# Layer norm tiles shared with GpSimd and ScalarE, and the first chunk's products of the upper halves put ahead of those of the lower halves

## The chip, the cores and the metric

One core of a Trainium2 chip runs the kernel. The metric is the device time of one execution in microseconds (us), the median of a few runs; lower is better. The engines work side by side, each through its own list of instructions, and meet at semaphores: TensorE (PE; its weight loads PEld), VectorE (DVE), ScalarE (ACT), GpSimd (POOL) and SyncE (SP, which issues the DMAs).

## The reference

Two transformer blocks of two layers each, on 256 tokens of width 1024. The change lies in the layer norms of the second block, and in the matmul that follows each of them (it also touches the matmul behind the RMS norms of the first block):

```python
def _layer_norm(x, g, b):
    xf = x.astype(jnp.float32)
    mu = jnp.mean(xf, axis=-1, keepdims=True)
    var = jnp.mean(jnp.square(xf - mu), axis=-1, keepdims=True)
    return ((xf - mu) * lax.rsqrt(var + LN_EPS) * g + b).astype(x.dtype)
...
    for l in range(DEPTH):
        x = _layer_norm(DN_ALPHA * x + 0.5 * _swiglu(x, ffn1_w1[l], ffn1_w2[l]), ln1_g[l], ln1_b[l])
        mix = _token_mix(x, w_in[l], ...)
        x = _layer_norm(DN_ALPHA * x + mix, ln2_g[l], ln2_b[l])
        x = _layer_norm(DN_ALPHA * x + 0.5 * _swiglu(x, ffn2_w1[l], ffn2_w2[l]), ln3_g[l], ln3_b[l])
```

The last of the six layer norms has no matmul behind it and is written elsewhere, so five are concerned.

## The kernel before

The tokens lie along the free dimension: `x[:, k, 0:256]` is tile k of eight (KT = 8), 128 model columns by 256 tokens in float32. All matmuls are made in float32r from halves: each operand is the sum of an upper half (rounded) and a lower half (what the rounding left), and a product takes three matmuls: upper weight with upper operand, upper weight with lower operand, lower weight with upper operand (`three`).

The weights come in chunks of 1 MB through a ring in SBUF. For each chunk ScalarE rounds it to `w_hi` (`round_next`, two halves of 1024 columns), VectorE makes the rest `w_lo` (`rest_next`, `rest_half`), and TensorE runs 48 matmuls over it. `w_hi` and `w_lo` hold two chunks, so chunk c+2 can be rounded once TensorE is done with chunk c.

A layer norm stands at the start of a stage; the mean, the squares and the root `rs` (the reciprocal of the standard deviation, 128x256, the same in all partitions) were made at the end of the stage before, by `Moments`. In `layer_norm` VectorE multiplies each tile with the gain and the root (`scaled_x`); ScalarE adds the bias and rounds to the upper half (`upper`); VectorE makes the lower half (`lower`); and after the eight tiles ScalarE adds the bias in place (`affine`). VectorE's list is written out as: tiles 0, 1, 2, then lower half 0, tile 3, lower half 1, and so on. TensorE runs the first chunk of the stage in `pe_side_by_side`: two output tiles side by side, and for each k the six matmuls of that tile as soon as its lower half is there.

Two kinds of stages begin so: `project_and_compress` (twice) and `ffn_stage` (three times). What ScalarE does next is, in the first, two copies of chunk 0's result out of PSUM and the rounding of chunk 2; in the second, the load of the table for Silu, the gate of chunk 0 and the rounding of chunk 2. The chunks 0 and 1 were rounded ahead.

In the first block the stage `glu_stage` (twice) starts with `model_norm`, and its first chunk runs through `pe_side_by_side` too; there GpSimd makes the upper halves and VectorE the lower ones.

Of the kernel before, what the change touches and what calls it, by code (L numbers as in the profile page):

```python
# [26 lines left out]
P = 128  # L27
D = 1024
KT = D // P
# [88 lines left out]
def build(nc, wstream, xT, ctxT, cT, consts, vecs, rpb, rel, out):  # L118
    ctx = ExitStack()
    with ctx:  # L120
# [80 lines left out]
        rows_turned = count("rows_turned")  # L201
        modulated = count("modulated")
        total_squares = count("total_squares")
        late_consts = count("late_consts")
        values_taken = count("values_taken")
        values_turned = count("values_turned")
# [117 lines left out]
                        mm.then_inc(half_read.sem, 1)  # L324
            mm.then_inc(chunk_done.sem, 1)

        def pe_side_by_side(pe, hi, lo, before, tok=S):

            pe_acc(pe, 0, 0)
            pe_half(pe, 0, 0, 1)  # L330
            for k in range(KT):
                before(k)
                for m in range(2):
                    mm = three(pe, acc(0, tok, m * 512), slice((m * KT + k) * P, (m * KT + k + 1) * P), g0[0] % 2,
                               hi(k), lo(k), k == 0, k == KT - 1)
            mm.then_inc(chunk_done.sem, 1)

        def pe_in_parts(pe, j, hi, lo, before, out):
# [231 lines left out]
        class Norm:  # L570
# [1 line left out]

            def __init__(self, pe, act, dve, before):
                self.pe, self.act, self.dve, self.before = pe, act, dve, before

        def model_norm(mod, scales, scratch):

            m0, u0, l0, s0 = mixed.n, upper.n, lower.n, scaled_x.n  # L580
            model_hi, model_lo = model_halves()

            def act_steps(act):
                for k in range(KT):
                    act.wait_ge(scaled_x.sem, s0 + k + 1)
                    for w in range(2):
                        v = scratch(k)[:, w * S:w * S + S]
                        o = act.activation(v, v, ACT.Identity, scale=scales[:, k, w:w + 1], bias=mod[:, k, w:w + 1])
                    o.then_inc(mixed.sem, 1)
                round_next(act, 0, 0)  # L590

            def pool_steps(pool):
                for k in range(KT):
                    pool.wait_ge(mixed.sem, m0 + k + 1)
                    pool.tensor_copy(model_hi[:, k, :], scratch(k)).then_inc(upper.sem, 1)

            def dve_steps(dve):
                for n in range(KT + 3):
                    if n < KT:
                        dve.tensor_tensor(scratch(n), x[:, n, :], rs[:], ALU.mult).then_inc(scaled_x.sem, 1)  # L600
# [9 lines left out]
            n = Norm(None, act_steps, dve_steps, lambda pe, k: pe.wait_ge(lower.sem, l0 + k + 1))  # L610
            n.pool = pool_steps
            return n

# [63 lines left out]
        def layer_norm(layer, which):  # L677

            gains, biases = par(layer, f"ln{which}_g"), par(layer, f"ln{which}_b")
            r0, s0, u0, l0 = rooted.n, scaled_x.n, upper.n, lower.n  # L680
            c = g0[0] + 1

            def src(k):
                return x[:, k, 0:S]

            def act_steps(act):
                for k in range(KT):
                    act.wait_ge(scaled_x.sem, s0 + k + 1)
                    act.activation(x_hi[:, k, 0:S], src(k), ACT.Identity, bias=biases[:, k:k + 1]
                                   ).then_inc(upper.sem, 1)  # L690
                for k in range(KT):
                    act.wait_ge(lower.sem, l0 + k + 1)
                    act.activation(src(k), src(k), ACT.Identity, bias=biases[:, k:k + 1]).then_inc(affine.sem, 1)

            def dve_steps(dve):
                dve.wait_ge(rooted.sem, r0)
                for n in range(KT + 2):
                    if n < KT:
                        dve.scalar_tensor_tensor(out=src(n), in0=src(n), scalar=gains[:, n:n + 1], in1=rs[:, 0:S],
                                                 op0=ALU.mult, op1=ALU.mult).then_inc(scaled_x.sem, 1)  # L700
                    k = n - 2
                    if 0 <= k < KT:
                        dve.wait_ge(upper.sem, u0 + k + 1)
                        dve.scalar_tensor_tensor(out=x_lo[:, k, 0:S], in0=src(k), scalar=biases[:, k:k + 1],
                                                 in1=x_hi[:, k, 0:S].bitcast(F32), op0=ALU.add, op1=ALU.subtract
                                                 ).then_inc(lower.sem, 1)
                rest_half(dve, c, 0, 1)

            for count_ in (scaled_x, affine, upper, lower):
                count_.n += KT  # L710
            return Norm(None, act_steps, dve_steps, lambda pe, k: pe.wait_ge(lower.sem, l0 + k + 1))

        scored = count("scored")
        sunk = count("sunk")
# [670 lines left out]
        def glu_stage(layer, pads, glu_gate, tok, norm, na_bias):  # L1385
# [11 lines left out]
            with nc.Block() as block:  # L1397
# [11 lines left out]
                @block.tensor  # L1409
                def _(pe):  # L1410
                    hi, lo = model_operand(tok)
                    keep_awake(pe, 9, 1536)
                    for j in range(n):
                        if j:
                            pe_columns(pe, j // 2, j % 2, hi, lo, tok)
                        else:
                            pe_side_by_side(pe, hi, lo, lambda k: norm.before(pe, k), tok)
# [404 lines left out]
        def ffn_stage(layer, norm, more=True, bias=None):  # L1822
# [10 lines left out]
            with ExitStack() as st:  # L1833
# [20 lines left out]
                with nc.Block() as block:  # L1854
# [7 lines left out]
                    def _(pe):  # L1862
# [4 lines left out]

                        def up_chunk(i, s):
                            if norm and first(i, s):
                                pe_side_by_side(pe, hi, lo, lambda k: norm.before(pe, k))  # L1870
# [98 lines left out]

                    @block.gpsimd  # L1970
                    def _(pool):
                        def chunk(i, s):
                            j = 2 * i + s
                            pool.wait_ge(acc_free.sem, g0[0] + s + 1 + 2 * i)
                            pool.tensor_copy(h_hi[:, j, :], hid[:, s, :]).then_inc(upper.sem, 1)  # L1975
                            pool.wait_ge(upper.sem, h0 + s + 1 + 2 * i)
                            pool.tensor_tensor(h_lo[:, j, :], hid[:, s, :], h_hi[:, j, :].bitcast(F32),  # L1977
                                               ALU.subtract).then_inc(lower.sem, 1)
                        pairs_of(pool, chunk)
# [462 lines left out]
        def project_and_compress(layer, plan, norm, kkc, vc, v_b, gates, st):  # L2442
# [44 lines left out]
            with nc.Block() as block:  # L2487
# [19 lines left out]

                @block.gpsimd
                def _(pool):
                    pool.memset(both[:].bitcast(F32), 0.0).then_inc(gpart.sem, 1)  # L2510
                    earlier = iter([(gpart.sem, gb + 1)] + [(values_flat.sem, f0 + k) for k in range(1, 8)])
                    flatten(pool, range(2, 4), values_flat, lambda: next(earlier))

                @block.tensor
                def _(pe):
# [22 lines left out]
                    for j, (kind, o, _) in enumerate(plan[:n]):  # L2538
                        if kind == "r":
                            pe_rows(pe, j // 2, j % 2, S, 256)  # L2540
                        elif j == 0:
                            pe_side_by_side(pe, *model_operand(S), lambda k: norm.before(pe, k))
# [517 lines left out]
```

## Time and profile before

| | us |
|---|---|
| median of 3 runs | 2368.11 (2368.05 to 2371.05) |
| the profiled execution | 2366.44 |
| its span in the trace | 2364.7 |

The profiled execution is 1.67 us below the median of the runs; its span is 1.74 us shorter than its time, which is what lies around the program. The mean granted TensorE clock was 0.997 of full speed. In the rows further down a time of the timeline counts from the start of the span; `x3` is three instructions that follow each other on an engine, with the time of all; what stands in brackets is how long the engine sat idle before, and what ended the wait.

### The profile page before, as it was taken

Reading aid. Unit: us, or ns where it says so; the run is one execution under the profiler, and the core shown is the slowest. Engines: PE = TensorE matmul, PEld = TensorE weight load, DVE = VectorE, ACT = ScalarE, POOL = GpSimd, SP = SyncE. Lnnn points to the kernel's source line nnn. Section 1 sums busy time; section 2 is a strip of 40 time slices with the busy share of each in tenths; the row PEclk is TensorE's granted clock in tenths of the full one; section 3 lists DMA queues with packets and bytes.
Section 4 is the critical chain, followed back from the end, with each engine's and each line's share of the span. In section 5 each row is a group of like instructions: output and inputs, shape, how many; then the busy total and the mean of one; then the engine's idle time right before and its main releaser. Section 6 shows DMA issues by size and latency. Waiting matters only on the chain. (4 is left out here: it accounts for less than half of the span.)

```text
span 2364.7 us, 45036 instructions
## 1 busy us (share of the span) xinstructions
PE 2275.5 (96%) x17296; PEld 2054.3 (87%) x17296; DVE 1498.9 (63%) x2663; ACT 1191.2 (50%) x1934; POOL 244.1 (10%) x272
## 2 busy tenths in 40 slices
PE   6999999999989999999999899999999998999998
PEld 3777677788878689999988899999999988999998
DVE  5487974453567875656476766665665577667654
ACT  6344743643345556434366555543544566555443
POOL 0012000000012000023010100131131001000320
PEclk9999999999999999999999999999999999999999
DMA  7321023434233035555554335455455453344552
GB/s 292 122 74 61 2 107 145 168 151 160 89 123 116 19 125 182 193 196 195 195 176 154 132 138 183 163 191 195 159 195 196 161 192 139 126 161 162 194 195 89
DMA packets 61844, 355.61 MB, mean 150 GB/s; under 512 B 6208, under 2 KB 19712, under 8 KB 20352
## 3 DMA queue, kind: packets, MB, share of 16 engines
q1 hardware_dynamic: 61552, 353.55, 41.7%
q8 instruction: 102, 1.67, 0.3%
q14 instruction: 46, 0.38, 0.1%
q10 hardware_dynamic: 144, 0.01, 0.0%
HBM read 349.29 MB, written 1.10 MB: 148 GB/s over the span
## 5 line engine op out<-in xcount | busy, mean ns | idle before, releaser
L257 DVE TENSOR_TENSOR w_lo<-ring,w_hi 128x1024 fp32r<-128x1024 f32 x638 | 812.3, 1306 | 441.1 <-ACT w_hi L243 440.6
L299 PE MATMUL psum<-halves,w_hi 128*128 128x256 f32 (+1 forms) x3314 | 1003.9, 303 | 12.7 <-DVE halves L604 3.7
L301 PE MATMUL psum<-halves,w_lo 128*128 128x256 f32 (+1 forms) x3314 | 985.4, 297 | 0.0
L300 PE MATMUL psum<-halves,w_hi 128*128 128x256 f32 (+1 forms) x3314 | 984.4, 297 | 0.0
L243 ACT ACTIVATE w_hi<-ring 128x1024 fp32r<-128x1024 f32 (+1 forms) x638 | 644.0, 1049 | 301.4 <-PE psum L301 134.5
L299 PEld LDWEIGHTS psum<-halves,w_hi 128*128 128x128 f32 x3314 | 624.1, 188 | 48.9 <-issue 11.5
L300 PEld LDWEIGHTS psum<-halves,w_hi 128*128 128x128 f32 x3314 | 624.3, 188 | 25.7 <-issue 1.7
L301 PEld LDWEIGHTS psum<-halves,w_lo 128*128 128x128 f32 x3314 | 623.6, 188 | 23.6
L1900 PE MATMUL psum<-h_hi,w_hi 128*128 (+1 forms) x640 | 176.6, 276 | 0.0
L1902 PE MATMUL psum<-h_lo,w_hi 128*128 (+1 forms) x640 | 176.6, 276 | 0.0
L1903 PE MATMUL psum<-h_hi,w_lo 128*128 (+1 forms) x640 | 176.6, 276 | 0.0
L1924 ACT ACTIVATE gate<-psum 128x256 f32<-128x256 f32 x88 | 33.9, 385 | 258.2 <-PE psum L301 258.2
L906 ACT ACTIVATE probT<-psum 128x512 f32<-128x512 f32 (+3 forms) x128 | 79.5, 621 | 149.1 <-PE psum L821 149.1
L1975 POOL CAST h_hi<-hid 128x256 f32 (+1 forms) x88 | 35.1, 399 | 994.8 <-DVE hid L1944 994.8
L921 ACT ACTIVATE prob<-prob,neg 128x256 f32<-128x256 f32 (+6 forms) x256 | 127.6, 502 | 19.2 <-DVE neg L874 18.1
L1900 PEld LDWEIGHTS psum<-h_hi,w_hi 128*128 128x128 f32 x640 | 120.1, 188 | 0.0
L1902 PEld LDWEIGHTS psum<-h_lo,w_hi 128*128 128x128 f32 x640 | 120.1, 188 | 0.0
L1903 PEld LDWEIGHTS psum<-h_hi,w_lo 128*128 128x128 f32 x640 | 120.1, 188 | 0.0
L1944 DVE SCALAR_TENSOR_TENSOR hid<-psum,gate 128x256 f32<-128x256 f32 x88 | 37.3, 424 | 125.5 <-ACT gate L1924 125.5
L1977 POOL TENSOR_TENSOR h_lo<-hid,h_hi 128x256 f32 (+1 forms) x88 | 111.2, 1264 | 13.5 <-POOL h_hi L1975 12.7
L1521 DVE SCALAR_TENSOR_TENSOR conv_out<-cpad,vec,conv_out 128x512 f32<-128x512 f32 (+1 forms) x180 | 108.6, 668 | 0.0
L821 PEld LDWEIGHTS psum<-cst,prob 128*128 128x128 f32 (+1 forms) x544 | 57.4, 138 | 48.8 <-DVE prob L881 39.5
(334 smaller groups left out, 2922.0 us busy)
## 6 DMA issues: line engine op xcount, KB each, us to landing
ring<-wstream SPq DMA_DIRECT2D x320, 1024.0 KB, 4.8
x<-xT SPq DMA_DIRECT2D x2, 1024.0 KB, 7.5
x<-ctxT SPq DMA_DIRECT2D x2, 1024.0 KB, 10.1
rel_bias<-bias_by_distance SPq DMA_DIRECT2D x2, 1024.0 KB, 7.5
fox_bias<-forgetting_sums SPq DMA_DIRECT2D x2, 1024.0 KB, 7.5
cst<-consts SPq DMA_DIRECT2D x1, 1534.0 KB, 11.7
wk<-wk_once SPq DMA_DIRECT2D x8, 128.0 KB, 4.4
kk_sw<-kk_sw SPq DMA_DIRECT2D x8, 128.0 KB, 5.7
```

Of the source, the lines that this page charges most:

```text
L243: act.activation(w_hi[:, c % 2, h], ring[:, (c + 2 * i) % RING, h], ACT.Copy).then_inc(hi_done.sem, 1)
L257: dve.tensor_tensor(w_lo[:, c % 2, h], ring[:, (c + 2 * i) % RING, h], w_hi[:, c % 2, h].bitcast(F32), ALU.subtract).then_inc(split_done.s ...
L299: pe.matmul(o, w_hi[:, c, w_cols], hi, start=first, stop=False)
L300: pe.matmul(o, w_hi[:, c, w_cols], lo, start=False, stop=False)
L301: return pe.matmul(o, w_lo[:, c, w_cols], hi, start=False, stop=last)
L906: act.activation(self.probT[0:w, v % self.TURNS, :, 0:n], psum[0:w, at:at + wide].rearrange("p (h k) -> p h k", h=2)[:, :, 0:n], ACT.Copy) ...
L921: o = act.activation(p, p, ACT.Exp, bias=self.neg[:, t % 3, half:half + 1], accum_out=self.den[:, t % 3, half:half + 1])
L1521: dve.scalar_tensor_tensor(out=o, in0=src, scalar=wc, in1=o, op0=ALU.mult, op1=ALU.add).then_inc(conv_step.sem, 1)
L1900: pe.matmul(o, w_hi[:, c, b:b + P], h_hi[:, kt, :], start=start and k == 0, stop=False)
L1902: pe.matmul(o, w_hi[:, c, b:b + P], h_lo[:, kt, :], start=False, stop=False)
L1903: mm = pe.matmul(o, w_lo[:, c, b:b + P], h_hi[:, kt, :], start=False, stop=False)
L1977: pool.tensor_tensor(h_lo[:, j, :], hid[:, s, :], h_hi[:, j, :].bitcast(F32), ALU.subtract).then_inc(lower.sem, 1)
```

## The change

VectorE scales tiles 0 to 4 as before. GpSimd multiplies tiles 5, 6 and 7 with the root, ScalarE then multiplies each of them with the gain (in place) and waits for its own result before it rounds the tile. In `pe_side_by_side` the four matmuls that need only the upper half of tile n (upper and lower weights, two output tiles) come as soon as that upper half is there, and the two that need the lower half of tile n-1 come behind them. That function also serves the two stages with `model_norm`.

```diff
         def pe_side_by_side(pe, hi, lo, norm, tok=S):
+            c = g0[0] % 2
...
             pe_acc(pe, 0, 0)
             pe_half(pe, 0, 0, 1)
-            for k in range(KT):
-                before(k)
-                for m in range(2):
-                    mm = three(pe, acc(0, tok, m * 512), slice((m * KT + k) * P, (m * KT + k + 1) * P), g0[0] % 2,
-                               hi(k), lo(k), k == 0, k == KT - 1)
+            for n in range(KT + 1):
+                if n < KT:
+                    norm.rounded(pe, n)
+                    for m in range(2):
+                        o = acc(0, tok, m * 512)
+                        pe.matmul(o, w_hi[:, c, columns_of(m, n)], hi(n), start=n == 0, stop=False)
+                        pe.matmul(o, w_lo[:, c, columns_of(m, n)], hi(n), start=False, stop=False)
+                k = n - 1
+                if k >= 0:
+                    norm.rest_made(pe, k)
+                    for m in range(2):
+                        mm = pe.matmul(acc(0, tok, m * 512), w_hi[:, c, columns_of(m, k)], lo(k), start=False,
+                                       stop=k == KT - 1)
             mm.then_inc(chunk_done.sem, 1)
...
         def layer_norm(layer, which):
...
+            OWN = 5
...
+            def pool_steps(pool):
+                pool.wait_ge(rooted.sem, r0)
+                for k in range(OWN, KT):
+                    pool.tensor_tensor(src(k), src(k), rs[:, 0:S], ALU.mult).then_inc(rooted_x.sem, 1)
+
             def act_steps(act):
                 for k in range(KT):
-                    act.wait_ge(scaled_x.sem, s0 + k + 1)
+                    if k < OWN:
+                        act.wait_ge(scaled_x.sem, s0 + k + 1)
+                    else:
+                        act.wait_ge(rooted_x.sem, o0 + k - OWN + 1)
+                        act.activation(src(k), src(k), ACT.Copy, scale=gains[:, k:k + 1]).then_inc(gained.sem, 1)
+                        act.wait_ge(gained.sem, n0 + k - OWN + 1)
                     act.activation(x_hi[:, k, 0:S], src(k), ACT.Identity, bias=biases[:, k:k + 1]
                                    ).then_inc(upper.sem, 1)
...
             def dve_steps(dve):
                 dve.wait_ge(rooted.sem, r0)
                 for n in range(KT + 2):
-                    if n < KT:
+                    if n < OWN:
                         dve.scalar_tensor_tensor(out=src(n), in0=src(n), scalar=gains[:, n:n + 1], in1=rs[:, 0:S],
                                                  op0=ALU.mult, op1=ALU.mult).then_inc(scaled_x.sem, 1)
...
@@ -1969,6 +2001,9 @@
                     @block.gpsimd
                     def _(pool):
+                        if norm:
+                            norm.pool(pool)
+
...
@@ -2507,6 +2542,7 @@
                 @block.gpsimd
                 def _(pool):
+                    norm.pool(pool)
                     pool.memset(both[:].bitcast(F32), 0.0).then_inc(gpart.sem, 1)
```

ScalarE's list at the start of the first `project_and_compress`, before (L689 makes the upper halves, `halves`; L693 is the bias in place; L2597 takes chunk 0's result out of PSUM; L243 rounds a half chunk):

```order
L689 ACTIVATE halves<-x,vec 128x256 [waits scaled_x] x8
L693 ACTIVATE x<-x,vec 128x256 [waits lower] x8
L2597 ACTIVATE x<-psum 64x2x256 [waits acc_free,chunk_done]
L2598 ACTIVATE x<-psum 64x2x256
L243 ACTIVATE w_hi<-ring 128x1024 [waits chunk_done,landed_odd]
```

and now (L715 is the rounding, L713 the gain, L719 the bias):

```order
L715 ACTIVATE halves<-x,vec 128x256 [waits scaled_x] x5
L713 ACTIVATE x<-x,vec 128x256 [waits rooted_x]
L715 ACTIVATE halves<-x,vec 128x256 [waits gained]
L713 ACTIVATE x<-x,vec 128x256 [waits rooted_x]
L715 ACTIVATE halves<-x,vec 128x256 [waits gained]
L713 ACTIVATE x<-x,vec 128x256 [waits rooted_x]
L715 ACTIVATE halves<-x,vec 128x256 [waits gained]
L719 ACTIVATE x<-x,vec 128x256 [waits lower] x8
L2633 ACTIVATE x<-psum 64x2x256 [waits acc_free,chunk_done]
```

Three instructions came in ahead of the last three roundings, each with a wait of ScalarE for itself behind it, and all that follows them stands behind them.

VectorE's list at the same place, now (L725 scales a tile, L730 makes a lower half; before, three more of the scalings alternated with the lower halves behind these):

```order
L725 SCALAR_TENSOR_TENSOR x<-x,vec,rs 128x256 [waits rooted]
L725 SCALAR_TENSOR_TENSOR x<-x,vec,rs 128x256 x2
L730 SCALAR_TENSOR_TENSOR halves<-x,vec,halves 128x256 [waits upper]
L725 SCALAR_TENSOR_TENSOR x<-x,vec,rs 128x256
L730 SCALAR_TENSOR_TENSOR halves<-x,vec,halves 128x256 [waits upper]
L725 SCALAR_TENSOR_TENSOR x<-x,vec,rs 128x256
L730 SCALAR_TENSOR_TENSOR halves<-x,vec,halves 128x256 [waits upper] x6
L258 TENSOR_TENSOR w_lo<-ring,w_hi 128x1024 [waits hi_done]
```

and GpSimd's, now (before, the memset was its first work there; in `ffn_stage` its first work was a cast behind the first gate):

```order
L2543 UNCONDITIONAL_BRANCH [waits barrier_Pool_Activation_PE_DVE_SP_gather]
L705 TENSOR_TENSOR x<-x,rs 128x256 [waits rooted]
L705 TENSOR_TENSOR x<-x,rs 128x256 x2
L2546 MEMSET both 128x4096
L2518 TENSOR_TENSOR flat<-x,vec 64x120 [waits gpart,doubled]
```

The first five scalings stand where they stood; GpSimd's three multiplications wait for the same semaphore as VectorE's first scaling, so both engines begin at once, and both read tiles of `x` and the root from SBUF.

## Rows read from the trace of the kernel before

**Rows 1.** Stretches: window; length; busy us of PE, PEld, DVE, ACT, POOL; granted clock; DMA.

```profile
1202.10:1212.00 9.90, 9.57 (x78) 9.35 (x79) 7.59 (x19) 7.86 (x18) 3.52 (x1) 1.00 0.41 133
...
2167.30:2177.30 10.00, 9.70 (x78) 9.48 (x79) 7.56 (x17) 8.00 (x17) 0.00 (x0) 1.00 0.40 125
...
1504.00:1590.00 86.00, 86.00 (x761) 86.00 (x760) 52.55 (x48) 38.64 (x50) 27.04 (x32) 1.00 0.53 194
```

**Rows 2.** Timeline of VectorE, second layer norm (a `ffn_stage`): start, duration.

```profile
1494.59 1.28 DVE L699 SCALAR_TENSOR_TENSOR x<-x,vec,rs 128x256 f32<-128x256 f32 x3 [0.91 <-PEq L2280]
...
1496.98 0.47 DVE L699 SCALAR_TENSOR_TENSOR x<-x,vec,rs 128x256 f32<-128x256 f32 x1
...
1499.75 1.27 DVE L704 SCALAR_TENSOR_TENSOR halves<-x,vec,halves 128x256 fp32r<-128x256 f32 x3
1500.93 1.22 DVE L257 TENSOR_TENSOR w_lo<-ring,w_hi 128x1024 fp32r<-128x1024 f32 x1
...
1506.26 2.90 DVE L257 TENSOR_TENSOR w_lo<-ring,w_hi 128x1024 fp32r<-128x1024 f32 x2 [0.53 <-ACT w_hi L243]
```

**Rows 3.** Timeline of ScalarE, the same stage.

```profile
1499.86 0.51 ACT L689 ACTIVATE halves<-x,vec 128x256 fp32r<-128x256 f32 x1 [0.29 <-DVE x L699]
1500.28 3.29 ACT L693 ACTIVATE x<-x,vec 128x256 f32<-128x256 f32 x8
1503.59 1.28 ACT L1924 ACT_TABLE_LOAD   x1
...
1505.17 2.00 ACT L243 ACTIVATE w_hi<-ring 128x1024 fp32r<-128x1024 f32 x2
```

**Rows 4.** Timeline of TensorE, the same stage: tile 5, chunk 1's first, chunk 2's first.

```profile
1500.30 0.37 PE L299 MATMUL psum<-halves,w_hi 128*128 128x256 f32 x1
...
1502.43 0.28 PE L317 MATMUL psum<-halves,w_hi 128*128 128x262 f32 x1
...
1507.87 0.28 PE L299 MATMUL psum<-halves,w_hi 128*128 128x256 f32 x1
```

**Rows 5.** Timeline of three engines, first layer norm (a `project_and_compress`); last: chunk 2's first matmul.

```profile
1202.19 1.28 DVE L699 SCALAR_TENSOR_TENSOR x<-x,vec,rs 128x256 f32<-128x256 f32 x3 [0.91 <-PEq L1854]
...
1212.30 2.01 ACT L243 ACTIVATE w_hi<-ring 128x1024 fp32r<-128x1024 f32 x2
...
1213.39 2.36 DVE L257 TENSOR_TENSOR w_lo<-ring,w_hi 128x1024 fp32r<-128x1024 f32 x2 [3.62 <-ACT w_hi L243]
...
1215.49 0.28 PE L299 MATMUL psum<-halves,w_hi 128*128 128x256 f32 x1
```

**Rows 6.** Timeline of POOL and DVE where both read SBUF (last row: POOL idle).

```profile
1014.73 1.81 POOL L1977 TENSOR_TENSOR h_lo<-hid,h_hi 128x256 fp32r<-128x256 f32 x1
...
1014.71 2.91 DVE L257 TENSOR_TENSOR w_lo<-ring,w_hi 128x1024 fp32r<-128x1024 f32 x2 [0.53 <-ACT w_hi L243]
...
1049.14 0.74 POOL L1977 TENSOR_TENSOR h_lo<-hid,h_hi 128x256 f32 x1 [0.17 <-POOL h_hi L1975]
...
1309.80 1.13 DVE L2739 SCALAR_TENSOR_TENSOR fox_bias<-fox_bias,c_col,cst 128x128 f32<-128x128 f32 x1
...
1315.50 0.34 DVE L2739 SCALAR_TENSOR_TENSOR fox_bias<-fox_bias,c_col,cst 128x128 f32<-128x128 f32 x1
```

**Rows 7.** Timeline of ScalarE: the root, its second step waits for its first.

```profile
1200.95 0.47 ACT L566 ACTIVATE rs<-psum,consts_small 128x256 f32<-128x256 f32 x1 [1.49 <-PE psum L651]
1201.45 0.42 ACT L568 ACTIVATE rs<-rs 128x256 f32<-128x256 f32 x1
```

**Rows 8.** Second `glu_stage`: a stretch (columns as rows 1), then timeline rows of two engines.

```profile
667.30:674.20 6.90, 6.58 (x26) 5.80 (x27) 6.90 (x10) 5.33 (x9) 4.08 (x12) 0.51 0.41 150
...
671.33 3.31 DVE L604 TENSOR_TENSOR halves<-nv,halves 128x512 fp32r<-128x512 f32 x4
...
676.16 2.75 PE L1426 MATMUL psum<-na_bias,cst 128*128 128x384 f32 x8
```

**Rows 9.** Timeline of TensorE, first `glu_stage`: first matmul behind its chunk 0.

```profile
67.58 0.59 PE L1426 MATMUL psum<-x,cst 128*128 128x384 f32 x1 [1.75 <-DMA x<-rpb]
```

More of the change, by code:

```diff
@@ L203, in build @@
         total_squares = count("total_squares")
+        rooted_x, gained = count("rooted_x"), count("gained")
         late_consts = count("late_consts")
@@ L325, in pe_columns, with pe_side_by_side, columns_of @@
             mm.then_inc(chunk_done.sem, 1)
-        def pe_side_by_side(pe, hi, lo, before, tok=S):
+        def pe_side_by_side(pe, hi, lo, norm, tok=S):
+            c = g0[0] % 2
+            def columns_of(m, k):
+                return slice((m * KT + k) * P, (m * KT + k + 1) * P)
             pe_acc(pe, 0, 0)
             pe_half(pe, 0, 0, 1)
-            for k in range(KT):
-                before(k)
-                for m in range(2):
-                    mm = three(pe, acc(0, tok, m * 512), slice((m * KT + k) * P, (m * KT + k + 1) * P), g0[0] % 2,
-                               hi(k), lo(k), k == 0, k == KT - 1)
+            for n in range(KT + 1):
[11 more added lines that the diff above has]
+                                       stop=k == KT - 1)
             mm.then_inc(chunk_done.sem, 1)
@@ L570, in build, with __init__ @@
         class Norm:
-            def __init__(self, pe, act, dve, before):
-                self.pe, self.act, self.dve, self.before = pe, act, dve, before
+            def __init__(self, act, dve, rounded, rest_made):
+                self.act, self.dve, self.rounded, self.rest_made = act, dve, rounded, rest_made
         def model_norm(mod, scales, scratch):
@@ L609, in model_norm @@
                 c.n += KT
-            n = Norm(None, act_steps, dve_steps, lambda pe, k: pe.wait_ge(lower.sem, l0 + k + 1))
+            n = Norm(act_steps, dve_steps, lambda pe, k: pe.wait_ge(upper.sem, u0 + k + 1),
+                     lambda pe, k: pe.wait_ge(lower.sem, l0 + k + 1))
             n.pool = pool_steps
@@ L679, in layer_norm @@
             gains, biases = par(layer, f"ln{which}_g"), par(layer, f"ln{which}_b")
-            r0, s0, u0, l0 = rooted.n, scaled_x.n, upper.n, lower.n
+            OWN = 5
+            r0, s0, u0, l0, o0, n0 = rooted.n, scaled_x.n, upper.n, lower.n, rooted_x.n, gained.n
             c = g0[0] + 1
@@ L707, in dve_steps @@
                 rest_half(dve, c, 0, 1)
-            for count_ in (scaled_x, affine, upper, lower):
+            for count_ in (affine, upper, lower):
                 count_.n += KT
-            return Norm(None, act_steps, dve_steps, lambda pe, k: pe.wait_ge(lower.sem, l0 + k + 1))
+            scaled_x.n += OWN
+            for count_ in (rooted_x, gained):
+                count_.n += KT - OWN
+            n = Norm(act_steps, dve_steps, lambda pe, k: pe.wait_ge(upper.sem, u0 + k + 1),
+                        lambda pe, k: pe.wait_ge(lower.sem, l0 + k + 1))
+            n.pool = pool_steps
+            return n
         scored = count("scored")
@@ L1416, in _ @@
                         else:
-                            pe_side_by_side(pe, hi, lo, lambda k: norm.before(pe, k), tok)
+                            pe_side_by_side(pe, hi, lo, norm, tok)
                         if j < 2:
@@ L1869, in up_chunk @@
                             if norm and first(i, s):
-                                pe_side_by_side(pe, hi, lo, lambda k: norm.before(pe, k))
+                                pe_side_by_side(pe, hi, lo, norm)
                             else:
@@ L2541, in _ @@
                         elif j == 0:
-                            pe_side_by_side(pe, *model_operand(S), lambda k: norm.before(pe, k))
+                            pe_side_by_side(pe, *model_operand(S), norm)
                         else:
```

## The prediction

> **What bounds the kernel now.** I read the stretches first. In the first ten microseconds of a stage that opens with a layer norm TensorE is busy almost all the time at a granted clock of 1.00, and behind them, to the stage's end, all the time: 86.00 of 86.00 us in the second of the five stages [rows 1] (the first and the last of the five stretches are shown; the others read alike). So TensorE sets the pace, and what is lost or won while the norm feeds it is lost or won for good, if nothing else comes last a little later.
>
> The timelines say what feeds it. Count from VectorE's first scaling (t = 0, at 1494.59 in the second stage and 1202.19 in the first [rows 2, 5]). VectorE issues one instruction per 0.40 us without a pause: three scalings take 1.28 us, each lasting 0.48, and the last three lower halves begin at 5.16 and end at 6.43 [rows 2]. The fifth scaling (tile 4) begins at 2.39. ScalarE rounds tile 7 from 5.27 to 5.78, adds the bias to eight tiles until 8.98, loads a table until 10.28, and rounds chunk 2 from 10.58 [rows 3]. TensorE starts tile 5 at 5.71, which is 0.07 behind that tile's lower half (5.16 + 0.48 = 5.64); from there on it runs without a wait: chunk 1 begins at 7.84 and chunk 2 at 13.28 [rows 4]. The 48 matmuls of chunk 1 took 5.44 us, 0.113 each. Six per tile are 0.68 us, and VectorE delivers a tile per 0.79 us: that is the little that feeding costs today, besides the start.
>
> The reader should also see the next thing that could come last. VectorE starts the lower half of chunk 2's weights at 11.67, and one takes 1.22 [rows 2], so the first is ready at 12.89; TensorE wants it at 13.28. The margin is 0.39 us, less the 0.07 in which TensorE gets going. In the other kind of stage the same step begins at 11.20 and TensorE begins chunk 2 at 13.30 [rows 5].
>
> **GpSimd beside VectorE.** The three multiplications that GpSimd takes over read two tiles in SBUF, at the moment at which VectorE works without a pause on tiles in SBUF. The trace has that encounter. A GpSimd subtraction of 128x256 takes 0.74 us by itself, and 1.81 when it begins just behind one of VectorE's; and two subtractions of VectorE, 2.36 us with GpSimd idle [rows 5], take 2.91 with one of GpSimd's between them [rows 6]. The engines take turns, one whole instruction each, and a turn of GpSimd costs VectorE 2.91 - 2.36 = 0.55 us. It holds for this form of instruction too: a SCALAR_TENSOR_TENSOR of VectorE took 1.13 us beside GpSimd and 0.34 with GpSimd done [rows 6]. The Trainium skill has a rule for it (SBUF — State Buffer, section "SBUF: two separate sides"): a VectorE instruction with two SBUF inputs and a GpSimd instruction that reads SBUF exclude each other for the whole of an instruction. By that rule alone a turn would cost all of GpSimd's instruction, and the sum below would be some 2.9 us more; the measured 0.55 decides.
>
> So VectorE's list loses three scalings (3 x 0.40 = 1.2 us), but these stood behind the fifth scaling, and the three turns (3 x 0.55 = 1.65 us) come ahead of it: GpSimd waits for the same root as VectorE and takes every second turn at once. Tile 4's scaling begins at 2.39 + 1.65 = 4.04, ends at 4.52, and ScalarE rounds tile 4 at 4.55 (0.03 behind, the gap that also stands between the two steps of the root [rows 7]).
>
> **ScalarE's chain.** From here ScalarE makes the last three tiles by itself: the gain, a wait for it, the rounding. An instruction of this size with an operand per partition issues per 0.40 us and lasts 0.49 (eight in 3.29 us [rows 3]); the wait adds 0.03. A tile takes 0.40 + 0.49 + 0.03 = 0.92 us. The gain itself is in no row; its bounds are 0.42 (without such an operand [rows 7]) and 0.51 (the rounding [rows 3]), and I take 0.49 as the nearest form. Tile 7 is rounded at 4.55 + 3 x 0.92 = 7.31, until 7.82; it was 5.27 to 5.78. ScalarE is 2.04 us late, and everything behind it in its list with it. GpSimd's own products are long there (three turns end near 2.5), so that wait costs nothing, and VectorE makes the lower half of tile 7 from 7.85 to 8.33.
>
> **TensorE.** The new order lets it start an upper half earlier, but the end is what counts: tile 7's four upper products start at 7.82 + 0.07 = 7.89, two lower ones of tile 6 and two of tile 7 follow, 8 x 0.113 = 0.91 us. Chunk 1 begins at 8.80 instead of 7.84 and would end at 14.24.
>
> Then chunk 2. In `ffn_stage` (three) the bias, the table, the gate and the rounding all move by 2.04, so the first part is ready at 12.89 + 2.04 = 14.93 and TensorE begins at 15.00 instead of 13.28: 1.72 us late, 0.76 of them a new wait. In `project_and_compress` (two) it is 11.20 + 2.04 + 1.22 + 0.07 = 14.53 instead of 13.30: 1.23. One chunk later ScalarE has caught up (a gate and a rounding are under 2.5 us of a chunk's 5.44), TensorE stays full, and nothing gives the time back.
>
> **The stages with `model_norm`.** Only TensorE's order changes. In the second one VectorE's lower halves end at 671.33 + 3.31 = 674.64, and chunk 0 ends at 676.16, 1.52 us later, since the granted clock was 0.51 for 6.9 us and TensorE had fallen behind [rows 8]. Now only a few lower products are left at 674.64; they end at 674.9 to 675.2. I credit 1.0 us (bounds: 0, if a later meeting of the engines takes it back, and 1.2). In the first one TensorE waits 1.75 us behind chunk 0 for a DMA [rows 9], which hides any gain: nothing.
>
> **The sum.** 3 x 1.72 + 2 x 1.23 - 1.0 = 6.6 us. On the profiled execution's 2366.44 that is 2373.0; on the median of the runs, 1.67 above it, 2374.7, which I forecast. Bounds: a turn of GpSimd between 0.55 and its whole 0.74 (+2.9 over fifteen turns), the gain between 0.42 and 0.51 (-1.0 to +0.3), the credit (+1.0 to -0.2). Together 5.4 to 10.8, or 2373.5 to 2378.9.
>
> **The rivals.**
> A, the engines don't block each other here. Then tile 4 is rounded at 2.90 and tile 7 at 5.66, still 0.39 later than before since ScalarE's 0.92 per tile is longer than VectorE's 0.79. TensorE ends chunk 0 at 6.17 + 0.07 + 0.91 = 7.15, 0.69 sooner, but chunk 2 is ready 0.39 later: in `ffn_stage` it begins at 13.35, 0.07 later than before; in the others at 12.88, 0.42 sooner. 3 x 0.07 - 2 x 0.42 - 1.0 = -1.6, or 2366.5: no change. Against it stand the five rows of rows 6; for it only that none shows these very operands.
> B, faster. As A, and the later ScalarE costs nothing, so that all five stages keep the 0.69 and the glu stage its 1.2: -4.6, or 2363.5. It decides if chunk 2's first part is ready before 7.15 + 5.44 - 0.07 = 12.52; even before the change it was ready at 12.89 [rows 2], so this would need ScalarE's gain to be nearly free.
> C, the clock falls. TensorE gets its tiles with gaps of up to half a microsecond at first. In the glu stage it was granted about half speed for 6.9 us [rows 8] after a stretch in which it mostly waited for its tiles. Were that to happen in the five stages, with tiles coming so that TensorE is busy seven tenths of the time (40 matmuls of 0.113 us between 1.6 and 7.9), some 43 matmuls would take 0.113 us more, 4.9 us, of which the gaps take up 2.1: 2.8 us per stage, in all 2389. Against it: seven tenths is far more than in that stretch.
> D, the extra edits cancel each other: GpSimd gets its turns only when VectorE pauses (near 4.4). Then its last product comes at 4.4 + 3 x 0.74 = 6.6, tile 7 is rounded at 7.15, and the sum is 5 x 0.16 less, 2373.9: the same side, inside the range.
>
> **Chances.** The forecast with its bounds, D among them, 0.82; A 0.10; B 0.04; C 0.04. About 0.2% (4.7 us) is what a measurement of this kernel tells from no change; the forecast lies 1.9 us above that bound, and I leave 0.09 of its 0.82 below it, for a smaller loss. Of A 0.01 goes to faster, for a gain that I don't see. So slower 0.73 + 0.04 = 0.77, same 0.09 + 0.09 = 0.18, faster 0.04 + 0.01 = 0.05. The range reaches from 2370.0, for losses cut by a third, to 2379.0, and leaves out A, B and C.
>
> **What the profile after would show.** Right: three GpSimd multiplications from t = 0, of which the later ones take over a microsecond; VectorE's second and third scalings some 1.0 us instead of 0.48; the last rounding near 7.3 and the bias until 11.0; TensorE starting chunk 1 near 8.8, and in `ffn_stage` a wait of 0.7 us on VectorE's `w_lo` ahead of chunk 2, at t = 15.0; clock 1.00 in all five; chunk 0 of the second glu stage done near 675. Wrong: scalings of 0.48 us beside GpSimd (A); a chain on ScalarE that is shorter than 0.92 per tile; TensorE at chunk 2 at its old time, which would say that something else feeds it; or a loss here that a later meeting of the engines takes back.

## The result, and the profile after

| | before | after |
|---|---|---|
| median of 10 runs each, same chip | 2368.39 us (2366.68 to 2371.05) | 2375.78 us (2373.47 to 2378.28) |
| ratio, 95% interval | | 1.0029 [1.0021, 1.0037] |
| the profiled execution, its span | 2366.44, 2364.7 | 2376.59, 2374.8 |
| granted clock of TensorE, mean | 0.997 | 0.995 |

The change costs 7.4 us; 6.6 were forecast on the median of the runs that stood there (2368.11 to 2374.7), and the time lies inside the range. All below counts from VectorE's first scaling (L725) of a stage, t = 0: 1497.88 in the second of the five stages, 1203.31 in the first.

First the stretches that answer to [rows 1], and one chunk-filled stretch behind them. Columns as there.

```profile
1203.22:1213.12 9.90, 9.64 (x69) 8.64 (x70) 8.12 (x16) 7.39 (x17) 5.94 (x4) 1.00 0.31 107
1497.79:1507.79 10.00, 9.75 (x71) 8.73 (x72) 8.10 (x14) 7.50 (x17) 2.47 (x3) 1.00 0.30 108
...
1512.80:1598.80 86.00, 86.00 (x758) 86.00 (x759) 53.18 (x49) 37.08 (x47) 28.40 (x33) 1.00 0.55 195
```

The clock was granted in full, so no time went there (it was 1.00 in all five). TensorE seems as busy as before, but in the ten microseconds it began 69 to 71 matmuls instead of 78 or 79: a matmul that comes after a gap lasts longer in the records (0.38 us instead of 0.28), and busy time hides what the count shows.

The timeline of VectorE, GpSimd and ScalarE in the second stage answers to [rows 2, 3]:

```profile
1497.85 2.47 POOL L705 TENSOR_TENSOR x<-x,rs 128x256 f32<-128x256 f32 x3 [179.91 <-POOLq L2315]
1497.88 2.73 DVE L725 SCALAR_TENSOR_TENSOR x<-x,vec,rs 128x256 f32<-128x256 f32 x3 [0.91 <-PEq L2315]
...
1501.72 0.47 DVE L725 SCALAR_TENSOR_TENSOR x<-x,vec,rs 128x256 f32<-128x256 f32 x1
...
1502.23 0.51 ACT L715 ACTIVATE halves<-x,vec 128x256 fp32r<-128x256 f32 x1 [0.28 <-DVE x L725]
1502.65 0.49 ACT L713 ACTIVATE x<-x,vec 128x256 f32<-128x256 f32 x1
1503.18 0.51 ACT L715 ACTIVATE halves<-x,vec 128x256 fp32r<-128x256 f32 x1
...
1505.06 0.51 ACT L715 ACTIVATE halves<-x,vec 128x256 fp32r<-128x256 f32 x1
1505.47 3.29 ACT L719 ACTIVATE x<-x,vec 128x256 f32<-128x256 f32 x8
...
1510.36 2.00 ACT L244 ACTIVATE w_hi<-ring 128x1024 fp32r<-128x1024 f32 x2
...
1511.45 2.90 DVE L258 TENSOR_TENSOR w_lo<-ring,w_hi 128x1024 fp32r<-128x1024 f32 x2 [0.52 <-ACT w_hi L244]
```

VectorE's first three scalings take 2.73 us instead of 1.28, while GpSimd's three multiplications take 2.47. After that VectorE runs at its old pace, so the 1.45 us are all that GpSimd costs it. ScalarE rounds tile 4 at 4.35 (1502.23) and tile 7 at 7.18, 0.94 us per tile in between, and carries its lateness through the bias to the rounding of chunk 2: t = 12.48, which was 10.58.

TensorE, answering to [rows 4]:

```profile
1506.64 0.28 PE L318 MATMUL psum<-halves,w_hi 128*128 128x262 f32 x1
...
1512.73 0.38 PE L300 MATMUL psum<-halves,w_hi 128*128 128x256 f32 x1 [0.48 <-DVE w_lo L258]
1512.95 0.29 PE L301 MATMUL psum<-halves,w_hi 128*128 128x256 f32 x1
```

Chunk 1 begins at 8.76 (before 7.84) and chunk 2 at 14.85 (before 13.28), behind a new wait for VectorE's `w_lo`. In the `project_and_compress` stages chunk 2 begins at 14.48 and 14.49.

The second `glu_stage`, answering to the last two of [rows 8]:

```profile
672.44 3.31 DVE L618 TENSOR_TENSOR halves<-nv,halves 128x512 fp32r<-128x512 f32 x4
...
676.14 2.75 PE L1458 MATMUL psum<-na_bias,cst 128*128 128x384 f32 x8
```

TensorE is done with chunk 0 at 3.70 us behind the first of VectorE's last four lower halves instead of 4.83.

### The profile page after: what moved, and what is told of

Read it like the earlier page. It is cut to its first block and busy times, and to the rows that moved or that the text cites. A ratio compares the mean times of both kernels' runs of the same rounds, so it can differ in the third digit from the quotient of the medians.

```text
span 2374.8 us, 45051 instructions
## 1 busy us (share of the span) xinstructions
PE 2287.6 (96%) x17296; PEld 2060.7 (87%) x17296; DVE 1499.1 (63%) x2648; ACT 1198.5 (50%) x1949; POOL 259.8 (11%) x287
## 3 DMA queue, kind: packets, MB, share of 16 engines
q8 instruction: 102, 1.67, 0.3%
## 5 line engine op out<-in xcount | busy, mean ns | idle before, releaser
L300 PE MATMUL psum<-halves,w_hi 128*128 128x256 f32 (+1 forms) x3202 | 966.8, 302 | 9.2 <-DVE w_lo L258 4.0
L302 PE MATMUL psum<-halves,w_lo 128*128 128x256 f32 (+1 forms) x3202 | 952.1, 297 | 0.0
L301 PE MATMUL psum<-halves,w_hi 128*128 128x256 f32 (+1 forms) x3202 | 951.5, 297 | 0.0
L300 PEld LDWEIGHTS psum<-halves,w_hi 128*128 128x128 f32 x3202 | 601.6, 188 | 41.9 <-issue 6.8
L301 PEld LDWEIGHTS psum<-halves,w_hi 128*128 128x128 f32 x3202 | 601.9, 188 | 25.2 <-issue 1.7
L302 PEld LDWEIGHTS psum<-halves,w_lo 128*128 128x128 f32 x3202 | 602.2, 188 | 22.5
```

The source lines that it names most:

```text
L300: pe.matmul(o, w_hi[:, c, w_cols], hi, start=first, stop=False)
L301: pe.matmul(o, w_hi[:, c, w_cols], lo, start=False, stop=False)
L302: return pe.matmul(o, w_lo[:, c, w_cols], hi, start=False, stop=last)
```

## The experiments

Theory: the loss is made of two delays in series, the turns that GpSimd takes ahead of tile 4, and ScalarE's chain of gain, wait and rounding for three tiles; the new order of TensorE by itself gains. Rivals: one of the two parts alone makes the loss (the turns, so that the chain is hidden; or the chain, which is too slow whatever GpSimd does); the new order does harm; or a fixed price falls due as soon as GpSimd takes part. Ratios are to the kernel before on the same chip. u7 is the rounding of tile 7, c1 and c2 the first matmuls of chunks 1 and 2, all as t in the second stage (in brackets: c2 in the first stage, a `project_and_compress`).

| kernel | median us (runs) | before us (runs) | ratio, interval | u7 | c1 | c2 |
|---|---|---|---|---|---|---|
| before | | | | 5.27 | 7.84 | 13.28 (13.30) |
| after | 2375.78 (10) | 2368.39 (10) | 1.0029 [1.0021, 1.0037] | 7.18 | 8.76 | 14.85 (14.48) |
| order_alone | 2365.59 (11) | 2367.80 (28) | 0.9991 [0.9982, 1.0000] | 5.27 | 6.97 | 12.94 (12.71) |
| split_alone | 2375.93 (6) | 2367.80 (28) | 1.0037 [1.0024, 1.0049] | 7.17 | 9.06 | 14.84 (14.76) |
| gpsimd_writes | 2368.55 (11) | 2367.80 (28) | 1.0001 [0.9992, 1.0010] | 5.73 | 7.32 | 13.40 (13.03) |
| no_gain | 2371.61 (11) | 2367.80 (28) | 1.0014 [1.0005, 1.0023] | 5.58 | 8.18 | 13.64 (13.83) |
| gpsimd_later | 2374.46 (9) | 2367.78 (25) | 1.0029 [1.0019, 1.0039] | 7.11 | 8.69 | 14.77 (14.40) |
| bias_later | 2373.77 (11) | 2367.78 (25) | 1.0026 [1.0017, 1.0035] | 7.18 | 8.77 | 14.22 (14.23) |
| order_bias_later | 2364.85 (11) | 2367.78 (25) | 0.9986 [0.9977, 0.9995] | 5.27 | 6.94 | 12.39 (12.40) |
| own7 | 2369.89 (11) | 2368.20 (17) | 1.0004 [0.9995, 1.0013] | 5.92 | 7.54 | 13.61 (13.25) |
| own6 | 2373.21 (7) | 2368.20 (17) | 1.0026 [1.0014, 1.0037] | 6.55 | 8.16 | 14.22 (13.86) |

**order_alone**: the new order of TensorE without the division of labour; VectorE scales all eight tiles.

```diff
-            OWN = 5
+            OWN = KT
...
-                        if norm:
-                            norm.pool(pool)
...
-                    norm.pool(pool)
```

> TensorE takes the upper products first, as in the changed kernel, but VectorE scales all eight tiles. My theory (GpSimd's turns and ScalarE's longer chain cost the time, the new order is good): chunk 1 begins about 1.1 us sooner in each of the five stages than before the change, as tile 7's lower half still ends at t = 6.43; but chunk 2 is bounded by ScalarE and VectorE, at t = 12.96 in the ffn stages (0.32 sooner) and 12.49 in the other two (0.81 sooner); with 1.1 in the second glu stage that is 3.7 us less than before: some 2364.7. Rival P (the new order itself costs the time): about 5 us or more above before.

Measured: 2365.59 us, 0.9991. The time fell by 2.2 us, by an interval that just reaches no change. Chunk 1 begins 0.87 sooner, but TensorE then waits at chunk 2 for the rest of the weights, as its timeline shows:

```profile
1502.52 0.28 PE L318 MATMUL psum<-halves,w_hi 128*128 128x262 f32 x1
...
1508.49 0.39 PE L300 MATMUL psum<-halves,w_hi 128*128 128x256 f32 x1 [0.35 <-DVE w_lo L258]
```

So the order doesn't harm these five stages, and in `ffn_stage` ScalarE's list (bias, table, gate, rounding) takes more than half of its gain away: 0.87 at chunk 1 are 0.34 at chunk 2.

**split_alone**: the division of labour, with the old order of TensorE.

```diff
-            for n in range(KT + 1):
...
+            for k in range(KT):
+                norm.rest_made(pe, k)
+                for m in range(2):
+                    mm = three(pe, acc(0, tok, m * 512), columns_of(m, k), c, hi(k), lo(k), k == 0, k == KT - 1)
```

> GpSimd and ScalarE take their part of tiles 5 to 7, but TensorE keeps the old order (six products per tile, behind its lower half). My theory: ScalarE's lateness sets chunk 2, as in the changed kernel, at t = 14.85 in the ffn stages and 14.5 in the others; without the gain in the glu stage 7.1 us above before, 2375.5. Rival P (the order costs the time): no change against before, 2368.4.

Measured: 2375.93 us, 1.0037, as expected. Chunk 2 in the second stage (t = 0 at 1496.35):

```profile
1511.19 0.39 PE L300 MATMUL psum<-halves,w_hi 128*128 128x256 f32 x1
```

The whole loss is the division's: chunk 1 is 0.3 later than with the new order, but chunk 2 begins at the same t in `ffn_stage` (14.84 and 14.85), since ScalarE's rounding decides there. In the first `project_and_compress` it begins at 14.76, 0.26 later than expected: TensorE, late at chunk 1, runs there without a wait.

**gpsimd_writes**: GpSimd writes a constant into tiles 5 to 7 instead of multiplying them, so that it reads nothing in SBUF; ScalarE's chain stays.

```diff
-                    pool.tensor_tensor(src(k), src(k), rs[:, 0:S], ALU.mult).then_inc(rooted_x.sem, 1)
+                    pool.memset(src(k), 0.5 + 0.1 * k).then_inc(rooted_x.sem, 1)
```

> As the changed kernel, but GpSimd writes a constant into tiles 5 to 7 instead of multiplying them with the root (the root is left out there), so that GpSimd reads nothing from SBUF. My theory: VectorE's scalings take 0.48 us again, ScalarE rounds tile 7 at t = 5.7 instead of 7.2, chunk 2 begins at 13.35 and 12.9, and the time is 1.7 us below before: 2366.7, no measurable change. Rival R (the turns cost nothing that counts, ScalarE's own chain does): as the changed kernel, 2375.8.

Measured: 2368.55 us, 1.0001. The timeline of GpSimd and VectorE:

```profile
1496.81 0.81 POOL L705 MEMSET x<- 128x256 f32 x3 [179.71 <-POOLq L2315]
1496.86 1.28 DVE L725 SCALAR_TENSOR_TENSOR x<-x,vec,rs 128x256 f32<-128x256 f32 x3 [0.91 <-PEq L2315]
```

VectorE's three scalings are back at 1.28, beside three GpSimd instructions at the same moment. So it is not GpSimd's being at work that costs VectorE 1.45 us; reading from SBUF is what the fill lacks. (It is also shorter than the multiplication, 0.31 us instead of 0.73, and does no arithmetic; this run doesn't separate the three.) The Trainium skill (SBUF — State Buffer, section "SBUF: two separate sides") has the reading as the condition: a VectorE instruction with two inputs in SBUF is shut out only by a GpSimd instruction that reads SBUF. The runs agree: 2.73 with reads, 1.28 without. The chain alone makes tile 7 0.46 later than before (5.73), and against the kernel before the loss is gone: it isn't the chain by itself.

**no_gain**: ScalarE's gain and its wait are left out for tiles 5 to 7; GpSimd's turns stay.

```diff
-                        act.activation(src(k), src(k), ACT.Copy, scale=gains[:, k:k + 1]).then_inc(gained.sem, 1)
-                        act.wait_ge(gained.sem, n0 + k - OWN + 1)
```

> As the changed kernel, but ScalarE leaves out the gain of tiles 5 to 7 and its wait for itself, and rounds them straight behind GpSimd. My theory: VectorE's turns remain (scalings near 0.95 us), tile 7 is rounded near t = 5.6, the bias is added until 9.25, chunk 2 begins near 13.2 in the ffn stages and 12.8 in the others: 2.3 us below before, 2366.1; so the turns alone cost little, and the loss needs both. Rival Q (the turns alone cost the time): as the changed kernel, 2375.8.

Measured: 2371.61 us, 1.0014: a loss where I expected a small gain. ScalarE's side came as expected (tile 7 at 5.58, the bias until 9.27), TensorE's didn't: chunk 1 began at 8.18 instead of 7.0.

```profile
1496.43 2.74 DVE L723 SCALAR_TENSOR_TENSOR x<-x,vec,rs 128x256 f32<-128x256 f32 x3 [0.91 <-PEq L2313]
...
1498.10 0.36 PE L342 MATMUL psum<-halves,w_hi 128*128 128x256 f32 x1
...
1504.61 0.28 PE L318 MATMUL psum<-halves,w_hi 128*128 128x262 f32 x1
```

I had counted only when the last tile comes. TensorE begins at 1.67, and its 48 matmuls are 5.44 us of work: without any further wait chunk 1 could begin at 7.11 at the earliest, and the early tiles come 0.87 us apart while VectorE is held up (its three scalings end at 2.74), where TensorE needs 0.68 for one. That, a restart behind each of these waits and a pace of 0.118 us per matmul instead of 0.113 make the rest. The turns alone therefore cost something at chunk 1 even if ScalarE catches up; chunk 2 is 0.36 late instead of 1.57.

**gpsimd_later**: GpSimd waits until VectorE has scaled tile 4, and multiplies only then.

```diff
-                pool.wait_ge(rooted.sem, r0)
+                pool.wait_ge(scaled_x.sem, s0 + OWN)
```

> As the changed kernel, but GpSimd starts its multiplications only when VectorE has scaled tile 4, so the turns come behind the five scalings. My theory (the turns cost because they stand ahead of tile 4; the rest is ScalarE's chain): the scalings take 0.48 us again, tile 7 is rounded at t = 6.1 instead of 7.2, the bias is added until 9.8, chunk 1 begins near 7.6 and chunk 2 at 13.8 in the ffn stages and 13.3 in the others: with the glu gain 0.4 us above before, about 2368.5, of the change's loss nearly all gone. Rival S (a turn costs the same wherever it stands): as the changed kernel, 2375.8.

Measured: 2374.46 us, 1.0029: a miss, almost the whole loss is still there. The timeline of the second stage (t = 0 at 1498.47):

```profile
1498.47 1.28 DVE L725 SCALAR_TENSOR_TENSOR x<-x,vec,rs 128x256 f32<-128x256 f32 x3 [0.91 <-PEq L2315]
...
1501.24 1.27 DVE L730 SCALAR_TENSOR_TENSOR halves<-x,vec,halves 128x256 fp32r<-128x256 f32 x3
...
1501.40 3.08 POOL L705 TENSOR_TENSOR x<-x,rs 128x256 f32<-128x256 f32 x3 [181.87 <-DVE x L725]
...
1503.15 0.51 ACT L713 ACTIVATE x<-x,vec 128x256 f32<-128x256 f32 x1 [1.28 <-POOL x L705]
```

VectorE's early scalings are quick again (1.28), so its delay was taken away as meant. But GpSimd's first product, begun at 2.93, is not there for ScalarE before 4.68: ScalarE stands idle for 1.28 us, and tile 7 comes at 7.11. By these times GpSimd was held up by VectorE's three lower halves and came through when VectorE ran out of work (1501.24 + 1.27 = 1502.51): of the 3.08 us the first product took 1.71, and the next two went by in 0.72 each. So the delay had only changed sides. The time is close to what rival S forecast, but for another reason: here ScalarE's chain began late for want of GpSimd's product.

**bias_later**: the changed kernel, with the bias in place (L719) moved behind the rounding of chunk 2 in ScalarE's list.

```diff
+            def bias_steps(act):
                 for k in range(KT):
                     act.wait_ge(lower.sem, l0 + k + 1)
...
                             if not (norm and first(i, s)):
                                 round_next(act, i, s)
+                            if norm and isinstance(i, int) and (i, s) == (0, 1):
+                                norm.bias(act)
```

> As the changed kernel, but ScalarE adds the bias in place only behind the rounding of chunk 2, so that its lateness does not reach chunk 2. My theory (two parts: TensorE's own late end of chunk 0, 0.95 us, and on top of it a wait for chunk 2): chunk 1 still begins at t = 8.8, chunk 2 without a wait at 14.3 to 14.4 instead of 14.85 and 14.48: 1.7 us less than the changed kernel, 2374.1. Rival T (ScalarE's lateness behind the norm is the whole cost): back near before, 2368.

Measured: 2373.77 us, 1.0026; its interval lies for the most part on that of the changed kernel, so the times alone don't tell the two apart. TensorE in the second stage (t = 0 at 1497.28), chunk 1's first and chunk 2's first:

```profile
1506.06 0.28 PE L318 MATMUL psum<-halves,w_hi 128*128 128x262 f32 x1
...
1511.50 0.28 PE L300 MATMUL psum<-halves,w_hi 128*128 128x256 f32 x1
```

The wait at chunk 2 is gone: it begins 14.22 - 8.77 = 5.45 behind chunk 1, as TensorE's own work wants. What remains is the lateness of chunk 1. So of the 1.57 us at chunk 2 in `ffn_stage` 0.63 came by ScalarE's list and 0.94 by the norm itself.

**order_bias_later**: both at once, the new order and the later bias, without the division of labour; it is the version that the other results point to.

> VectorE scales all tiles, TensorE takes the upper products first, and ScalarE adds the bias behind the rounding of chunk 2. My theory: chunk 1 begins at t = 7.06 as with the order alone, and chunk 2 without a wait at 12.5 to 12.7 in all five stages, 0.3 us sooner than the order alone in the three ffn stages: 1.0 us less than that kernel, about 2364.6, some 3 us below before. Rival: the table load and the gate still come last, no change against the order alone, 2365.6.

Measured: 2364.85 us, 0.9986 [0.9977, 0.9995], the lowest ratio here; the times alone don't tell it from order_alone. ScalarE and TensorE in the second stage (t = 0 at 1493.51):

```profile
1498.78 0.51 ACT L715 ACTIVATE halves<-x,vec 128x256 fp32r<-128x256 f32 x1 [0.28 <-DVE x L727]
1499.31 1.28 ACT L1960 ACT_TABLE_LOAD   x1
...
1500.93 2.00 ACT L244 ACTIVATE w_hi<-ring 128x1024 fp32r<-128x1024 f32 x2
...
1502.83 3.29 ACT L721 ACTIVATE x<-x,vec 128x256 f32<-128x256 f32 x8
...
1505.90 0.28 PE L300 MATMUL psum<-halves,w_hi 128*128 128x256 f32 x1
```

Chunk 2 is rounded at 7.42 instead of 10.58, so its rest is there long before TensorE wants it, and chunk 2 begins at 12.39 without a wait: the order's gain of 0.9 us per stage arrives whole at chunk 2.

**own7 and own6**: the changed kernel with one tile, and with two, given away instead of three.

```diff
-            OWN = 5
+            OWN = 7
```

> The changed kernel with one tile given away instead of three: GpSimd scales tile 7 alone and ScalarE gives it its gain; the new order of TensorE is kept. By the theory of the turns (one turn of 0.47 us ahead of tile 4, and one tile of ScalarE's chain at 0.94 us instead of three): tile 7 is rounded at about 5.9 us, chunk 1 begins at about 7.4 us and chunk 2 at about 13.5 us behind a feed-forward (before: 7.84 and 13.3), and the time is about 2367, which is the kernel before within its noise. A cost that comes whole as soon as GpSimd takes part in the stage would give nearly the changed kernel's 2375.

> The changed kernel with two tiles given away instead of three: GpSimd scales tiles 6 and 7, ScalarE gives them their gain. By the theory of the turns: tile 7 is rounded at about 6.5 us, chunk 1 begins at about 8.0 us and chunk 2 at about 14.2 us behind a feed-forward, and the time is about 2370, halfway between the order alone (2365.6) and the changed kernel (2375.8). A cost that comes whole with GpSimd's first instruction would give about 2375; one that lies only in the third tile would leave it at about 2366.

Measured: 2369.89 us, 1.0004, and 2373.21 us, 1.0026. The first scalings and GpSimd's share in own7, then in own6:

```profile
1498.20 0.73 POOL L705 TENSOR_TENSOR x<-x,rs 128x256 f32<-128x256 f32 x1 [178.91 <-POOLq L2315]
1498.23 1.78 DVE L725 SCALAR_TENSOR_TENSOR x<-x,vec,rs 128x256 f32<-128x256 f32 x3 [0.92 <-PEq L2315]
```

```profile
1497.31 1.60 POOL L705 TENSOR_TENSOR x<-x,rs 128x256 f32<-128x256 f32 x2 [179.42 <-POOLq L2315]
...
1497.34 2.25 DVE L725 SCALAR_TENSOR_TENSOR x<-x,vec,rs 128x256 f32<-128x256 f32 x3 [0.91 <-PEq L2315]
```

Three scalings of VectorE take 1.28, 1.78, 2.25 and 2.73 us with none, one, two and three of GpSimd's multiplications: 0.50, 0.47 and 0.48 for a turn. Tile 7 is rounded at 5.27, 5.92, 6.55 and 7.18, and chunk 2 begins at 12.94, 13.61, 14.22 and 14.85: 0.61 to 0.67 per tile given away, in even steps. There is no fixed price. The times of own7 and own6 lie 2.9 and 3.2 us above their expectations, and that of own6 can't be told from that of the changed kernel by the intervals; its trace says that chunk 2 begins 0.63 sooner than there. The even steps rest on the traces, not on the times.

**before_again**: the kernel before, unchanged, for a second profile.

> The kernel before once more, for a second profile. Both theories expect the same stages (chunk 1 at t = 7.85, chunk 2 at 13.3). The question is which differences between the profiles don't come from the change: where the granted clock falls to half, and whether the chunks behind the first norm take 5.44 us or 5.65.

Measured: 2366.66 us. Chunk 2 began at 13.30 in the second stage, as before; in the first one at 13.56, where the first profile had 13.30. The half-clock stretches lay elsewhere too (last section).

## Why the prediction was right

**The turns.** Step as put: a turn of GpSimd costs VectorE 0.55 us, three come ahead of tile 4, which is rounded at 4.55. Measured: 2.73 - 1.28 = 1.45 us, 0.48 each, tile 4 rounded at 4.35. The mechanism is the one forecast; gpsimd_writes, where GpSimd only fills, shows none of the delay. The size came from instructions four times as long [rows 6], and was 0.07 too large; 0.48 also lies below the bounds of 0.55 to 0.74 that it was given. Rival A (no blocking) is out, and with it B, which rests on it; so is C, since the clock was 1.00 in all five stages. Rival D (GpSimd gets in only when VectorE pauses) is not what happened here, but it is what happened in gpsimd_later; the time there, 2374.46, is close to the 2373.9 that D was given.

**ScalarE's chain.** As put: 0.92 us per tile, tile 7 at 7.31, ScalarE 2.04 late. Measured: 0.94 per tile (the gain lasts 0.49, the value chosen between the bounds), tile 7 at 7.18, ScalarE 1.90 late (12.48 for 10.58).

**Chunk 1** at 8.80: measured 8.76 to 8.79. The late tile 7 costs less than forecast, and a restart of TensorE behind each wait costs a little more.

**Chunk 2** at 15.00 in `ffn_stage` and 14.53 in `project_and_compress`: measured 14.85 and 14.48. The shifts are 1.57 (forecast 1.72) and 1.18 (1.23). The sentence that TensorE then stays full and gives nothing back held.

**The second glu stage**, credited with 1.0 us: 1.13 in the two profiled executions. In the three profiles with the old order TensorE ended chunk 0 at 4.47 to 4.83 behind the first of VectorE's last four lower halves, in all nine with the new order at 3.70 to 3.72, whether the clock had fallen there or not. So the credit is 0.8 to 1.1, and it is real.

**The first glu stage**, put at nothing, because TensorE waits there for a DMA that hides any gain. In the changed kernel's profile that is nearly so. In the other eight profiles with the new order it isn't: TensorE ends chunk 0 sooner, waits longer, and is then granted half its clock (the lower of its two levels). The eight matmuls behind the wait and the stretch 68.00 to 70.00, before, then in order_alone:

```profile
67.58 2.86 PE L1426 MATMUL psum<-x,cst 128*128 128x384 f32 x8 [1.75 <-DMA x<-rpb]
...
68.00:70.00 2.00, 2.00 (x9) 1.18 (x7) 2.00 (x2) 0.84 (x1) 0.00 (x0) 1.00 0.98 410
```

```profile
66.58 4.54 PE L1458 MATMUL psum<-x,cst 128*128 128x384 f32 x8 [2.97 <-DMA x<-rpb]
...
68.00:70.00 2.00, 2.00 (x5) 1.09 (x4) 0.07 (x1) 0.00 (x0) 0.00 (x0) 0.50 1.01 422
```

In these eight the matmuls take 4.2 to 5.5 us, and VectorE's first rest of the weights behind the end of chunk 1 begins 25.35 to 27.52 us behind the first of its last four lower halves of this stage, where the three profiles with the old order have 24.24 to 24.64 and the changed kernel's has 23.89. So in this stage the new order mostly loses 0.7 to 3.3 us, about what it gains in the second one, or more. It fits that order_bias_later, whose trace has 0.9 us in each of the five stages and 0.8 to 1.1 in the second glu stage, gained only 2.9 us on the medians; but the medians' share isn't shown, for there is one profile of each kernel, and how many of the changed kernel's ten runs lost time here isn't known.

**The sum.** 3 x 1.57 + 2 x 1.18 - 1.13 = 5.9 us, against 6.6 forecast and 7.4 measured on the medians (5.0 to 8.8 by the interval). One term was missing inside the five stages. A wait costs TensorE more than the wait: behind it the first matmul of chunk 2 lasts 0.38 us instead of 0.28, and the second begins 0.22 behind it instead of 0.113, so that the chunk takes 5.56 us instead of 5.44 [rows 4]. Besides, TensorE ran some chunks at 0.118 us per matmul instead of 0.113, in both kernels. At chunk 3 the five stages stand 1.47, 1.69, 1.88, 1.00 and 1.61 later than in the profile before, 7.6 in all, less 1.13 is 6.5. The forecast of 6.6 was thus near for the wrong reason in one respect: turns taken too dear made up for the restart that was left out. That part is luck. (The range's lower end, 2370.0, stands for a loss of 1.9 us; that is a loss cut to less than a third, and not by a third as the prediction has it.)

The two profiled executions differ by 10.1 us, which is more than the medians. 1.12 of it is there ahead of the first norm (1203.31 for 1202.19), the glu stage's credit included.

**Point by point in the experiments**, the two parts of the loss can't be had apart at their sum. With the new order and all eight tiles on VectorE, chunk 2 begins at 12.94 (`ffn_stage`); the chain alone makes it 13.40, the turns alone 13.64, both 14.85. The chain alone costs 0.46 because it starts on time and hides most of itself; behind the turns it starts late and is laid bare whole. This rests on the traces: in the ratios the chain alone costs 0.0010 over order_alone, the turns alone 0.0023 and both 0.0038, and with intervals of about 0.001 to either side 0.0038 can't be told from the sum, 0.0033.

What stays open: why the engines alternated, one instruction each, when both were released at the same moment (changed kernel, own6), and why GpSimd was kept out behind three instructions of VectorE in gpsimd_later. GpSimd began 0.03 us ahead of VectorE in the one and 0.16 behind it in the other; no run here varied that alone.

## What to carry to other kernels

Moving work from a busy VectorE to an idle GpSimd was no gain here, where both read SBUF at the same moment: price the move by what a turn costs the engine that keeps the pace, and look whether the turns fall ahead of the work that is needed first. A chain on another engine costs little while it starts on time, and all of itself once something ahead of it is late, so two costs that are each small may have to be added in series. And when work comes sooner at one meeting of the engines, see what is late at the next one: here the bias in place, which nothing waited for, stood ahead of the rounding that TensorE needed, and moving it is what let the new order's gain arrive whole at chunk 2. A wait that is said to hide a gain wants a look too: in the first glu stage the longer wait was followed by half the clock.

## What the runs showed of the hardware that was not expected

- GpSimd at work beside VectorE cost it nothing where it only wrote: three fills of 128x256 in 0.81 us beside three scalings in 1.28, the time without GpSimd.
- The same multiplication of GpSimd took 0.73 us when it went first (own7), 0.72 with VectorE idle (gpsimd_later), 0.91 in turns with VectorE, and 1.71 when it met three VectorE instructions in a row (gpsimd_later).
- Stretches of 48 matmuls took 5.44 or 5.65 us at a granted clock of 1.00, 0.113 or 0.118 per matmul, and which one changed from execution to execution of the same kernel: behind the first norm it was 5.44 in the first profile of the kernel before and 5.65 in the second. The cause was not found.
- TensorE was granted half its clock for a few microseconds at places that changed between executions; the place in the first glu stage (above) is the one that mostly goes with the new order. The kernel before, in the stretch from 226.60 to 230.20 of its first profile and of its second:

```profile
226.60:230.20 3.60, 3.03 (x31) 2.13 (x31) 2.67 (x14) 3.07 (x7) 0.00 (x0) 1.00 0.00 0
```

```profile
226.60:230.20 3.60, 3.14 (x24) 2.29 (x20) 2.68 (x12) 3.60 (x10) 0.00 (x0) 0.53 0.00 0
```
